# Moving the ring of split weights by 64 bytes, and the last SBUF region by 256 bytes, in a two-block transformer kernel

## What is computed

```python
# block 1: adaptive norms, Fourier mixing, latent attention over 512 + 256 keys, gates, MLP
mod_x = silu(c) @ ada_w + ada_b
hx = modulate(rmsnorm(x, norm1_g), sh1, sc1)
px = hx @ w_in                                  # 512 x 1024 by 1024 x 2976
att_x = latent_attention(qx, k_all, v_all)      # 8 heads
y_x = (g_f * (fourier_mix(fx) @ w_fourier) + g_a * (att_x @ w_mla_o)) @ w_out
x = x + g1 * y_x
x = x + g2 * square(relu(h2 @ w_up)) @ w_down   # 1024 -> 4096 -> 1024
# block 2: convolution and mLSTM, then a mixture of experts
z = rmsnorm_2(x) @ w_in_2 + b_in_2              # 1024 -> 3080
x = x + concat(conv_branch, mlstm_branch) @ w_out_2
# 32 experts of 1024 -> 512 -> 1024, two per token
x = x + sum_over_two(gate * (silu(xs @ w_gate[e]) * (xs @ w_up[e])) @ w_down[e])
return rmsnorm_2(x, final_norm_g)
```

## Time and profile before

| | |
|---|---|
| median of 3 runs | 1701.88 us (1701.83, 1701.88, 1703.94) |
| the profiled execution | 1704.96 us, its span 1703.2 us |
| mean granted TensorE clock | 0.972 |
| PE, weight loads (PEld), DVE, ACT busy | 96%, 78%, 75%, 54% of the span |
| experts' weights | 192 loads of 1 MB |
| the split: ACT L1515 | 256 of 1911 ns on average |
| the split: DVE L2176 | 256 of 2302 ns on average |

### The profile page before, as it was taken

One profiled execution on the slowest core, in us unless ns is written; L12 is line 12 of the kernel. 1 busy time (PEld: TensorE's weight loads), 2 busy tenths in 40 slices (PEclk: granted clock), 3 DMA queues, 4 the chain that ended last, 5 costly groups with the idle time before them and its releaser, 6 DMA issues.

```text
span 1703.2 us, 20092 instructions
## 1 busy us (share of the span) xinstructions
PE 1628.6 (96%) x8178; PEld 1321.0 (78%) x8178; DVE 1270.7 (75%) x1457; ACT 922.1 (54%) x1070; POOL 255.1 (15%) x176
## 2 busy tenths in 40 slices
PE   5999998999999999999999999899999999999994
PEld 2767876657888989898888777788888888888883
DVE  6554865786667847474799965589998999989994
ACT  6423235443343625262633234578788887888874
POOL 0000021000018333310000100102212122121110
PEclk9999998999999999999999989799999999999997
DMA  9106721003222324131222101299999999999993
GB/s 383 72 0 233 285 111 75 0 0 124 75 99 74 124 75 136 69 142 50 84 90 75 47 28 55 109 378 405 369 376 381 369 367 372 357 376 357 386 359 115
DMA packets 54482, 322.89 MB, mean 190 GB/s; under 512 B 12529, under 2 KB 13041, under 8 KB 17778
## 3 DMA queue, kind: packets, MB, share of 16 engines
q1 hardware_dynamic: 42192, 304.76, 47.0%
q0 software_dynamic: 9216, 8.43, 2.2%
q10 hardware_dynamic: 2978, 8.37, 1.3%
HBM read 323.60 MB, written 23.07 MB: 204 GB/s over the span
## 4 chain that ended last, share of the span: by engine, by line
PE 87%; DVE 6%; DMA 3%; ACT 3%; issue 1%; SPq 0%; POOL 0%; ACTq 0%; POOLq 0%; DVEq 0%
PE ps L584 26%; PE ps L1437 19%; PE ps L1464 10%; PE ps L1070 7%; PE ps L763 3%; PE ps L739 2%; PE ps L1326 2%; PE ps L1002 2%; DVE scr L2486 2%; PE ps L796 1%; PE ps L1423 1%; ACT whi L1515 1%; DMA xT<-in_x 1%; DVE wlo L2176 1%; PE ps L719 1%; PE ps L866 1%
## 5 line engine op out<-in xcount | busy, mean ns | idle before, releaser
L2176 DVE TENSOR_TENSOR wlo<-raw,whi 128x2048 fp32r<-128x2048 f32 x256 | 583.8, 2302 | 131.8 <-ACT whi L1515 131.6
L1515 ACT ACTIVATE whi<-raw 128x2048 fp32r<-128x2048 f32 x256 | 485.4, 1911 | 150.9 <-PE ps L584 41.6
L1437 PE MATMUL ps<-whi,xH 128*128 128x512 f32 x512 | 205.5, 401 | 1.4 <-DVE xL L2285 1.4
L1437 PE MATMUL ps<-whi,xL 128*128 128x512 f32 x512 | 201.8, 394 | 0.0
L1437 PE MATMUL ps<-wlo,xH 128*128 128x512 f32 x512 | 200.2, 391 | 0.0
L584 PE MATMUL ps<-hH,whi 128*128 128x512 f32 x352 | 140.6, 400 | 0.3 <-ACT dmax L1991 0.3
L584 PE MATMUL ps<-hL,whi 128*128 128x512 f32 x352 | 139.1, 395 | 0.0
L584 PE MATMUL ps<-hH,wlo 128*128 128x512 f32 x352 | 139.1, 395 | 0.0
L3217 POOL DMA_INDIRECT sum_scratch<-yb,idt x32 | 51.1, 1595 | 455.6 <-ACT yb L2116 420.2
L1437 PEld LDWEIGHTS ps<-whi,xL 128*128 128x128 f32 x512 | 96.7, 189 | 22.6
L1437 PEld LDWEIGHTS ps<-whi,xH 128*128 128x128 f32 x512 | 97.0, 189 | 20.6 <-DVE xL L2285 1.8
(11 more groups left out here) (514 smaller groups left out, 3525.1 us busy)
## 6 DMA issues: line engine op xcount, KB each, us to landing
raw<-in_experts SPq DMA_DIRECT2D x192, 1024.0 KB, 8.2
raw<-in_streamed SPq DMA_DIRECT2D x92, 1024.0 KB, 4.8
xT<-in_x SPq DMA_DIRECT2D x1, 2048.0 KB, 17.3
h_scratch<-hN ACTq DMA_DIRECT2D x4, 512.0 KB, 2.6
sum_scratch<-xN ACTq DMA_DIRECT2D x1, 2048.0 KB, 12.9
out<-Y SPq DMA_DIRECT2D x4, 512.0 KB, 2.7
ctxT<-in_ctx SPq DMA_DIRECT2D x1, 1024.0 KB, 18.7
Y<-sum_scratch SPq DMA_DIRECT2D x2, 512.0 KB, 5.6
```

The lines of the kernel that those rows point to most:

```text
L1437: ins = e.matmul(b.t[:, :], l, w, start=(kk == 0 and i == 0), stop=(kk == 7 and i == 2))
L1515: e.activation(u.hi, u.raw, ACT.Copy).then_inc(*p.inc("hi", n, on="hi"))
L2176: e.tensor_tensor(u.lo, u.raw, u.hi.bitcast(F32), ALU.subtract).then_inc(*p.inc("lo", n, on="lo"))
```

## The change

Two numbers of the SBUF map and one offset that depends on them. The region of the ring of split weights begins 16 floats (64 bytes) later. The last region `PH` begins 64 floats (256 bytes) later; the place `PH + 15456` of one early unit's low part is the same memory as `PH + 15520` before. `O_HH` and `O_RAW` stay. No instruction, wait or queue is added, removed or moved.

```diff
-    O_HH, O_CST, O_SCR, O_RST, O_RAW, O_HL, PH = 4096, 12288, 13648, 14672, 15184, 21328, 33616
+    O_HH, O_CST, O_SCR, O_RST, O_RAW, O_HL, PH = 4096, 12288, 13648, 14672, 15184, 21344, 33680
 ...
-    FIRST_HALF = {8: (PH, PH + 2048), 9: (PH + 4096, PH + 15520)}
+    FIRST_HALF = {8: (PH, PH + 2048), 9: (PH + 4096, PH + 15456)}
```

## The result

The changed kernel takes 1716.51 us (median of 6 runs, 1714.47 to 1716.93); the kernel before, run beside it, 1702.12 us (6 runs, 1701.68 to 1704.49). The ratio is 1.0078, with a 95% interval of 1.0067 to 1.0088. The forecast was 1705.6 us and its range ended at 1711.5. So the change makes the kernel slower, by 11 to 15 us, and by more than I allowed for.

The account below looks back on a forecast made before the run. The prediction took TensorE (PE), busy 96% of the span, as the bound. Its six terms summed to +3.7 us, which on the median of 1701.88 us made 1705.6 us, with a range of 1695.0 to 1711.5.

Parts of the forecast that it names:

- The mechanism: TensorE's pace goes with streamed minus stationary address, called distance, in 64-byte steps modulo 4; 226.7 to 233.3 ns at 512 columns.
- What I cost at nothing: ACT's and DVE's split, loads, stores of `Y`, the experts' fourth place (distance 1) and attention operands: no time in the sum.
- Term 2: `PH` tiles over the ring, 512 columns, 912 matmuls, distance 0 to 3: 226.7 to 233.3 ns, +6.1 us.
- term 1: `hH` over the ring, 512 columns, 1416 matmuls, distance 3 to 2: 233.3 to 231.1 ns, -3.1 us (bounds -9.4 and 0).
- term 3: Experts' three ring places, 512 columns, 1728 matmuls, distance 1 to 2: 228.9 to 231.1 ns, +3.8 us (-3.8 and +7.6).
- the line: Unseen distance 2 lies between 1 and 3: 231.1 ns for 512 columns, 115.6 for 256; 1705.6 us, chance 0.36.
- term 5: `hH` over the ring, 256 columns, 816 matmuls, distance 3 to 2: 113.3 to 115.6 ns, +1.8 us (0 and +5.5).
- term 6: `value`, the ring over `hH`, 192 matmuls, distance 1 to 2: 117.8 to 115.6 ns, -0.4 us (-0.9 and +0.4).
- Term 4: `PH` tiles over the ring, 256 columns, 672 matmuls, distance 0 to 3: 120.0 to 113.3 ns, -4.5 us.
- B: Rival: distance 2 costs as much as distance 3; sum +8.3 us, 1710.2 us, chance 0.13.
- A: Rival, two banks: the remainder counts modulo 2 only, distance 2 costs what 0 does; -5.7 us, 1696.2 us, chance 0.25.
- Rival C: Pace goes with row counts, tile order or stretch start, not the address; no change, 1701.9 us, chance 0.15.

Follow-up runs that it names:

- kernel 1: Kernel before with the ring at 21376 and `PH` at 33664, putting all dense-layer and expert pairs at distance 0; 1694.78 us, ratio 0.9949.
- kernel 2: Kernel before with the ring where the change puts it (21344) and `PH` at 33632, so `PH` tiles stay at distance 0 from it; 1711.76 us, ratio 1.0056.
- kernel 5: Kernel before with ring (21360) and `PH` (33648) at remainder 3: `hH` over ring at distance 1, ring over `xH`, `aH`, `hH` at 3; 1707.97 us, ratio 1.0023.
- kernel 3: Kernel before with `PH` alone moved by 256 bytes, the ring staying; 1704.09 us, ratio 1.0004.
- kernel 4: Kernel before with its whole slab moved 64 bytes, no distance between its tiles changed; 1702.88 us, ratio 0.9995.
- kernel 10: Kernel before with `TH` and `TL` alone moved by 48 floats, so all of `seven` stands at distance 3; 1703.88 us, ratio 0.9999.
- kernel 6: Kernel before with the ring 32 bytes past remainder 0 (21384) and `PH` at remainder 0 (33728); 1714.73 us, ratio 1.0066.
- kernel 7: Kernel before with 512-column pairs at distance 0 (`fm`, `att` at 1), MLP blocks moved 16 floats (`seven` at 3), ring places 4160 floats apart; 1690.64 us, ratio 0.992.
- kernel 8: Kernel before with ring and `PH` placed as in kernel 1, and `TH` and `TL` moved 48 floats to distance 3; 1691.16 us, ratio 0.9925.

## Why the prediction was wrong, point by point

- **What bounds the kernel**: right. PE is busy in the experts for 520.7 of 522 us after as before, and each ns of a matmul arrived.
- **The mechanism**: right for 128 rows and 512 columns. Distances go with the paces (kernels 1, 2, 5), moving one operand by a whole 256 bytes does nothing (kernel 3), and absolute alignment is nothing (kernel 4). With 256 columns the distance alone doesn't fix the pace (kernel 10), and the attention's scores stay at 233.3 ns at distance 0 (kernel 1).
- **What I cost at nothing**: right for ACT's and DVE's split (1915 and 2303 ns). The fourth place of the experts, left alone at distance 1, took 0.8 ns more, +0.4 us. The start times tell where: behind a unit in the ring's places its first five matmuls take 234, 234, 233, 232 and 229 ns in the mean (before: 231, 226, 229, 232, 226), and later ones 227 to 230. The dearer neighbour reaches into it, as in kernel 6.
- **Term 2**, the one with rows on both sides and 512 columns: +6.1 predicted, +5.9 measured.
- **Terms 1 and 3, "and take the point on the line, 231.1 and 115.6": this step failed.** Distance 2 takes 232.4 to 232.5 ns with 512 columns. 1.4 ns more on 1416 + 1728 matmuls is +4.4 us, of which the classes above show 3.7 (2.0 in term 1, 1.7 in term 3). Kernel 6 shows why: there is no line to stand on.
- **Terms 5 and 6**: distance 2 takes 118.8 ns with 256 columns and not 115.6, +1.6 us more than the +1.8 of the sum, inside its bounds; `value` gave +0.1 instead of -0.4. That width has no line either: 120.0, 117.8, 118.8 and 113.3 to 117.8 for the four distances.
- **Term 4, "Distance 3 has rows"**: it had, but I took one of two paces for the only one. The same trace held 113.5 and 117.9 ns at distance 3 (L739 and L719, above), and the earlier trace rows are six starts. The term gave back 2.0 us instead of 4.5: after the change `TH` stands at 3 beside `hH` at 2 and reaches 116.3. I gave it no bounds at all, since I took a pace for a property of one pair; kernel 10 shows that it isn't.
- **The base**: the terms were 8.5 us short (3.7 against 12.2), the forecast 10.9. Of the 8.5, distance 2 on the line is 5.8 (terms 1, 3, 5 and 6), term 4 2.5 and the fourth place 0.4, and term 2 was 0.2 too high. Nearly all of the rest is the base. I set the sum on the median of three runs, 1701.88, rather than on the profiled execution, which is 3.1 us higher; the classes, on the other hand, sum to 0.8 us more than the 11.4 between the two profiled executions. In the later runs the kernel before had medians of 1702.1 (6 runs, these three among them), 1703.4 (19), 1703.3 (15) and 1704.0 (13): the median of three was the lowest of these.
- **The rivals and the range**: B (distance 2 as dear as 3) was right for 512 columns, where most of the money is, and got 0.13. It had for it "nothing but that 2 and 3 are neighbours", and I tied the two widths together in it (113.3 for 256, which would save 0.9 us on `value` and cost nothing in term 5). Taken each at its own upper bound, the terms give 0 + 6.1 + 7.6 - 4.5 + 5.5 + 0.4 = +15.1 us and 1717.0. The prediction had written those bounds down and then ended the range at 1711.5, at a rival's time. Had it reached to the bounds, it would have held the 1716.5. A, the other side, fell with the first look at distance 2: its 226.7 ns against 232.5. Rival C had the attention's last head for it, and kernel 1 leaves that unexplained.

## What to carry to other kernels

Where PE is the bound, compare the paces of matmuls of one shape in the chain of waits, and several stretches of each. If they differ, move one operand's base by 64 bytes at a time and look for the fast one: here putting all pairs at the same remainder modulo 256 bytes is worth 0.5%, and the best mix (kernels 7 and 8, 1690.6 and 1691.2 us) 0.8% over the kernel before and 1.5% over the changed one (which ran in another group of runs), with no instruction changed. A rounder address of one buffer was no gain by itself here; the two operands must agree. In a forecast, an unseen case between two seen ones keeps both ends until a run has shown it, and each unknown keeps its own: three points on a line are three points.

## What the runs showed of the hardware

Pace in ns from start to start, 128 x 128 weights, at a granted clock of 0.99 to 1.00; distance in bytes modulo 256 between what is streamed and what is stationary:

| distance | 512 columns | 256 columns |
|---|---|---|
| 0 | 226.7 | 120.0 |
| 32 | 233.3 | 116.7 (`value`) |
| 64 | 228.9 | 117.8 |
| 128 | 232.4 to 232.5 | 118.4 to 118.9 |
| 192 | 233.3 | two paces, 113.3 to 114.1 and 117.8; 115.8 in `value` (kernel 5) |
| 224 | 233.3 | 118.3 |

A spread of 2.9% with 512 columns, and of 6% with 256, where distance 0, the fastest with 512, is the slowest. It holds with either operand stationary, and it doesn't depend on where the pair stands as a whole. Which part of the machine does it no run here shows. Three limits:

- Matmuls of 96 or 97 rows and 512 columns take 232.5 to 233.3 ns at distance 0 too (before and kernel 1).
- What ran before reaches in. At distance 0 the pace settles at 226.7 ns only after some eleven matmuls behind transposes (kernel 1) and after seven behind a unit at distance 32 bytes (kernel 6). With 256 columns it can change a whole stretch (kernel 10).
- The paces are means of patterns. At distance 128 `hH` over the ring takes 228 to 242 ns from one matmul to the next (L584 in after). At 192 bytes it takes mostly 230, 231, 235 or 236 (before). At distance 0 it is even to 1 ns.
